# Delta rule stage: decay and beta rows by DMA, a blockwise transpose for the second inverse, one product for keys with keys and queries

## The reference

```python
cum = jnp.cumsum(g, axis=-1)
decay = jnp.exp(jnp.where(causal, cum[..., :, None] - cum[..., None, :], -jnp.inf))
k_beta = k * beta[..., None]
a = jnp.where(strict, jnp.einsum('bhnid,bhnjd->bhnij', k_beta, k) * decay, 0.0)
rhs = jnp.concatenate([v * beta[..., None], k_beta * jnp.exp(cum)[..., None]], axis=-1)
sol = lax.linalg.triangular_solve(a + eye, rhs, left_side=True, lower=True, unit_diagonal=True)
u, w = sol[..., :dv], sol[..., dv:]
attn = jnp.einsum('bhnid,bhnjd->bhnij', q, k) * decay
q_dec = q * jnp.exp(cum)[..., None]
k_dec = k * jnp.exp(cum[..., -1:] - cum)[..., None]
def step(state, xs):
    v_new = u_c - jnp.einsum('bhck,bhkv->bhcv', w_c, state)
    o = jnp.einsum('bhck,bhkv->bhcv', q_c, state) + jnp.einsum('bhij,bhjv->bhiv', attn_c, v_new)
    state = state * last_c[..., None, None] + jnp.einsum('bhck,bhcv->bhkv', k_c, v_new)
    return state, o
```

## Time and profile before

| | us |
|---|---|
| median of 3 runs | 4228.07 (4224.93 to 4230.5) |
| the profiled execution | 4243.35 |
| its span, first to last instruction | 4241.6 |
| delta rule rounds 0 to 8 in it | 2069 to 3003 |
| a full round (start of one `keys_twice` copy on POOL to the next) | 118.5 to 123.2 |

### The profile page before, as it was taken

How to read it: one execution, slowest core, us unless ns; L and a number is a source line. 1 busy time by engine, 2 the same in 40 slices (tenths; PEclk the granted TensorE clock), 3 DMA queues, 4 the chain that set the end, 5 groups by cost and what they waited for, 6 DMA issues and landing times.

```text
span 4241.6 us, 62565 instructions
## 1 busy us (share of the span) xinstructions
PE 3905.2 (92%) x25559; PEld 3618.2 (85%) x25559; DVE 2563.3 (60%) x5015; ACT 1553.4 (37%) x2769; POOL 754.8 (18%) x613
## 2 busy tenths in 40 slices
PE   7999989889979999998899999999889999978999
PEld 5667869889979999988798888889789998978999
DVE  4654337889958999998455555555453423555342
ACT  4554223335533333333433333332242424444231
POOL 0000005556722333331211101111000001110000
PEclk9999999999989999999789999999899999998999
DMA  3112224448869999996001111110022221112221
GB/s 110 60 60 70 90 75 131 135 147 283 277 213 326 336 333 332 327 330 219 25 26 31 36 39 33 36 36 31 31 81 85 95 70 46 60 45 71 93 90 66
DMA packets 203069, 528.19 MB, mean 125 GB/s; under 512 B 17032, under 2 KB 91272, under 8 KB 202784
## 3 DMA queue, kind: packets, MB, share of 16 engines
q1 hardware_dynamic: 99792, 341.22, 24.1%
q0 software_dynamic: 37440, 136.33, 9.1%
q10 hardware_dynamic: 65552, 46.64, 3.5%
HBM read 477.99 MB, written 46.14 MB: 124 GB/s over the span
## 4 chain that ended last, share of the span: by engine, by line
PE 64%; DVE 24%; ACT 6%; issue 3%; DMA 1%; POOL 0%; DVEq 0%; ACTq 0%; POOLq 0%; SPq 0%
PE bank L94 63%; DVE wl L121 5%; DVE acc L131 3%; DVE H L121 2%; DVE row L163 2%; ACT wh L115 2%; DVE yc L131 1%; DVE eq L121 1%; PE bank L97 1%; DVE aal L121 1%; DVE fs L121 1%; DMA raw<-in_v 1%; DVE sq L131 1%; ACT Xh L115 1%; DVE Xl L121 1%
## 5 line engine op out<-in xcount | busy, mean ns | idle before, releaser
L94 PE MATMUL bank<-Xh,wh 128*128 128x272 f32 (+3 forms) x3680 | 1242.1, 338 | 63.1 <-ACT ft L115 27.0
L94 PE MATMUL bank<-Xl,wh 128*128 128x272 f32 (+3 forms) x3680 | 1174.0, 319 | 0.0
L94 PE MATMUL bank<-Xh,wl 128*128 128x272 f32 (+3 forms) x3680 | 1172.4, 319 | 0.0
L121 DVE TENSOR_TENSOR wl<-raw,wh 128x1024 fp32r<-128x1024 f32 (+1 forms) x536 | 574.4, 1090 | 463.9 <-ACT wh L115 462.8
L115 ACT ACTIVATE wh<-raw 128x1024 fp32r<-128x1024 f32 (+1 forms) x632 | 589.1, 953 | 700.1 <-PE bank L94 659.6
L94 PEld LDWEIGHTS bank<-Xh,wh 128*128 128x128 f32 x3680 | 720.1, 196 | 133.2 <-issue 63.9
L94 PEld LDWEIGHTS bank<-Xh,wl 128*128 128x128 f32 x3680 | 718.4, 195 | 21.0
L94 PEld LDWEIGHTS bank<-Xl,wh 128*128 128x128 f32 x3680 | 721.0, 196 | 17.0 <-issue 0.3
L121 DVE TENSOR_TENSOR H<-H,bank 128x384 f32<-128x384 f32 (+3 forms) x522 | 252.4, 493 | 339.0 <-PE bank L94 335.4
L94 PE MATMUL bank<-aah,wh 128*128 128x384 f32 x1024 | 356.1, 348 | 43.5 <-DVE wl L121 23.5
L121 POOL TENSOR_TENSOR wl<-raw,wh 128x1024 fp32r<-128x1024 f32 x96 | 274.3, 2859 | 518.5 <-ACT wh L115 518.4
(11 more groups left out here) (309 smaller groups left out, 6404.8 us busy)
## 6 DMA issues: line engine op xcount, KB each, us to landing
raw<-in_u SPq DMA_DIRECT2D x128, 512.0 KB, 4.1
raw<-in_v SPq DMA_DIRECT2D x128, 512.0 KB, 5.8
raw<-in_up SPq DMA_DIRECT2D x64, 512.0 KB, 3.6
raw<-in_down SPq DMA_DIRECT2D x64, 512.0 KB, 3.5
scratch<-gb ACTq DMA_DIRECT2D x12, 2048.0 KB, 13.8
gj<-scratch SPq DMA_DIRECT2D x32, 768.0 KB, 7.3
raw<-in_w_gdn SPq DMA_DIRECT2D x48, 512.0 KB, 3.5
raw<-in_w_att SPq DMA_DIRECT2D x36, 512.0 KB, 3.5
```

Source lines behind the costliest of these rows:

```text
L94: return Issued(self, self.q and self.q.matmul(out, l, r, start=start, stop=stop), 1)
L121: return Issued(self, self.q and self.q.tensor_tensor(out, a, b, op), 1)
```

## The change

It makes three edits in the levels, and an order that goes with them.

1. Rows by DMA. After the gates, ACT writes the rows of cumulated gates, of their exponentials and of the betas to a scratch tensor in HBM (`rows_out`). SP reads them back, spread over 128 partitions: `rows_in(p, g)` straight into DD and QE, `beta_in(p, g)` into one of the two `sq` buffers that the norms use elsewhere. PE's `decay` and the beta part of `pair_kk` are gone, ACT's exponential into TA and POOL's mask step too; DVE subtracts the column and adds the mask with one instruction a chunk (nine of 128x128 in place of three of 128x384), POOL multiplies the queries into QE in place.
2. One product. Keys and queries lie interleaved in one tile QK, and one matmul a chunk with the weights KD2 gives both, 128 columns.
3. The second inverse by transposes. "pd", its subtraction, and `level0` on PE and ACT are gone. After each update of TB, DVE transposes it in blocks of 32x32 into TA (`squares`, STREAM_TRANSPOSE, 128x384), five times a group. Blocks of up to 32 are all that levels 1 to 5 read.

The levels have 37 units of weight in `merge` in place of 45. Cut to its core:

```diff
+    def squares(self, out, in_):
+        return Issued(self, self.q and self.q.transpose(out, in_), 1)
...
-        QS = Ring([alloc("q", 9, 64) for _ in range(2)])
-        KS = Ring([alloc("k", 9, 64) for _ in range(3)])
+        QK = alloc("qk", 5, 9, 64)
+        QS = Ring([QK[:, i, :, :] for i in (1, 3)])
+        KS = Ring([QK[:, i, :, :] for i in (0, 2, 4)])
...
+            for p in range(2):
+                for g in range(3):
+                    rows_in(p, g)
+            beta_in(0)
+            beta_in(1)
...
         def levels_gdn(p):
-            DD.take(p), TB.take(p), KE.take(p), QE.take(p)
+            TB.take(p), KE.take(p)
             do("keys_twice", p)
             for g in range(3):
-                PA.take(("dec", p, g))
                 do("decay", p, g)
-                PA.give(("dec", p, g), ("dd", p, g, 0))
+            yield 1
+            for g in range(3):
+                for n in ("kk", "vt"):
+                    PA.take((n, p, g))
+                do("pair", p, g)
+                PA.give(("kk", p, g), ("attn", p, g))
+                PA.give(("vt", p, g), ("bv", p, g))
+                SQ.give(("beta", p, g), ("bb", p, g, 1))
+                beta_in(3 * p + g + 2)
                 yield 1
...
+                if c % 3 == 2 and p < 6:
+                    rows_in(p + 2, c // 3)
...
-                streams.append((levels_gdn(t - 1), 45))
+                streams.append((levels_gdn(t - 1), 37))
...
+            def pair(p, g):
                 ps = PS[clear(pe, PA, ("kk", p, g))]
                 pe.wait_ge("kd", p)
-                k = KS.at[p]
+                pe.wait_ge("qk", p, 0, 1)
+                first, second = sorted((2 * KS.slot[p], 2 * QS.slot[p] + 1))
                 for n in range(3):
-                    i = pe.mm(ps[:, n * 64:n * 64 + 64], KD2[:, 3 * g + n, :], k[:, 3 * g + n, :])
+                    i = pe.mm(ps[:, n * 128:(n + 1) * 128].rearrange("p (e i) -> p e i", e=2),
+                              KD2[:, 3 * g + n, :], QK[:, first:second + 1:second - first, 3 * g + n, :])
...
             def decay(p, g):
+                dd = DD.at[p]
+                dv.wait_ge("dup", 1, 1)
+                dv.wait_ge(f"rows{(3 * p + g) % 2}", p, g, 1)
+                for c in range(3 * g, 3 * g + 3):
+                    dv.stt(dd[:, c, :], dd[:, c, :], CC[:, c, p:p + 1], CS["mask"], ALU.subtract, ALU.add).then_inc(
+                        "dd", p, c)
...
+                dv.wait_ge("tmm", p, lv, g)
+                dv.tt(to, to, pt, ALU.subtract).then_inc("tb", p, lv, g)
                 if lv < 5:
-                    dv.wait_ge("dmm", p, lv, g)
-                    less("pd", "dmm", TA, 0).then_inc("ta", p, lv, g)
-                dv.wait_ge("tmm", p, lv, g)
-                less("pt", "tmm", TB.at[p], b).then_inc("tb", p, lv, g)
+                    dv.wait_ge("tb", p, lv, g)
+                    dv.squares(three(TA, g).rearrange("p c x -> p (c x)"), tb).then_inc("ta", p, lv, g)
...
+            def rows_in(p, g):
+                m = 3 * p + g
+                name = f"rows{m % 2}"
+                if p < 2:
+                    sp.wait_ge("dup", 3, 1)
+                    sp.wait_ge("nbe", 0)
+                    sp.wait_ge("rows_out", 2)
+                else:
+                    sp.wait_ge("so", p - 2, 3 * g + 2)
+                if m > 1:
+                    sp.wait_ge(name, (m - 2) // 3, (m - 2) % 3, 1)
+                for i, x in enumerate((DD.at[p], QE.at[p])):
+                    sp.dma(three(x, g), scratch3[i, 3 * g:3 * g + 3, 2 * p:2 * p + 2, :].rearrange(
+                        "c h i -> c (h i)").partition_broadcast(128)).then_inc(name, p, g, i)
```

More of the change, by code:

```diff
@@ L318, in __init__, with build @@
         self.name, self.i = name, i
-def build(nc, X, out, scratch, scratch2):
+def build(nc, X, out, scratch, scratch2, scratch3):
     ctx = ExitStack()
@@ L1178, in build, with beta_in @@
         QE, DD, TB, KE = (Ring([alloc(n, 9, 128) for _ in range(2)], given=gates_done) for n in ("qe", "dd", "tb", "ke"))
+        for pair in range(8):
+            QE.at[pair], DD.at[pair] = QE.bufs[pair % 2], DD.bufs[pair % 2]
+        def rows_in(p, g):
+            do("rows_in", p, g)
+        def beta_in(m):
+            if m < 24:
+                SQ.take(("beta", m // 3, m % 3))
+                do("beta_in", m // 3, m % 3)
         assert top[0] >= end
@@ L1311, in levels_gdn @@
         def levels_gdn(p):
[L1312 removed]
+            TB.take(p), KE.take(p)
             do("keys_twice", p)
             for g in range(3):
[L1315 removed]
                 do("decay", p, g)
[L1317 to L1333 removed]
+            yield 1
[7 more added lines that the diff above has]
+                beta_in(3 * p + g + 2)
+                yield 1
+            QS.give(p, ("kk", p, 2), ("qe", p, 2))
             for g in range(3):
@@ L2022, in pe_program @@
                 onehot=onehot, ba=ba,
-                gdn_dup=gdn_dup, decay=decay, pair_kk=pair_kk, pair_kq=pair_kq, keys_out=keys_out, level0=level0,
+                gdn_dup=gdn_dup, pair=pair, keys_out=keys_out,
                 level_x=level_x, level_t=level_t, scan_r=scan_r, scan_v=scan_v, scan_s=scan_s, ml_if=ml_if,
@@ L2807, in decay, with rows_out @@
             def decay(p, g):
[L2808 to L2820 removed]
+                ac.wait_ge("dd", p, 3 * g + 2)
+                ac.act(three(DD.at[p], g), three(DD.at[p], g), ACT.Exp).then_inc("dd_exp", p, g)
+            def rows_out():
+                ac.wait_ge("cum", 0)
+                ac.act(RR[1], CUM, ACT.Exp).then_inc("ecum", 0)
+                ac.wait_ge("ecum", 0)
+                for i, x in enumerate((CUM, RR[1], RB)):
+                    ac.dma(scratch3[i].rearrange("c h i -> h c i"), x).then_inc("rows_out", i)
             def scan_v(p, c):
@@ L3001, in decay, with pair @@
             def decay(p, g):
-                dd = DD.at[p]
-                po.wait_ge("dd", p, g, 0)
-                po.tt(three(dd, g), three(dd, g), b3(CS["mask"]), ALU.add).then_inc("ddm", p, g)
-            def pair_kq(p, g):
-                qe = clear(po, QE, p)
+                qe = QE.at[p]
                 q = QS.at[p][:, 3 * g:3 * g + 3, :].unsqueeze(2).to_broadcast([128, 3, 2, 64])
                 po.wait_ge("qk", p, 0, 1)
-                po.wait_ge("ec", p, g)
-                po.tt(four(qe, g), q, four(TA, g), ALU.mult).then_inc("qe", p, g)
-            def keys_out(p, g):
+                po.wait_ge(f"rows{(3 * p + g) % 2}", p, g, 1)
+                po.tt(four(qe, g), q, four(qe, g), ALU.mult).then_inc("qe", p, g)
+            def pair(p, g):
                 tb = clear(po, TB, p)
@@ L3185 @@
     scratch2 = nc.dram_tensor("scratch2", (4 * AHEAD, 128, NT), F32, kind="Internal").ap()
-    build(nc, X, out, scratch, scratch2)
+    scratch3 = nc.dram_tensor("scratch3", (3, 9, 16, 64), F32, kind="Internal").ap()
+    build(nc, X, out, scratch, scratch2, scratch3)
     r = run(nc, [{"in_" + n: a for n, a in arr.items()}], core_ids=[0])
```

123 lines of the change are left out of this document (42 added, 81 removed).

## The result

The changed kernel takes 4184.32 us (median of 4 runs, 4180.28 to 4191.06), the kernel before, measured beside it, 4229.28 (4224.93 to 4232.13). The ratio is 0.9896, 95% interval 0.9879 to 0.9913: 45 us less, 1.0%. The forecast was 4118, from 4064 to 4178: right in sign, and 66 us too low.

What follows compares the result with a forecast made beforehand. The prediction took TensorE (PE) to bound the levels stage; 133 us off PE, less 16 for new waits, 2 for betas and 5 for the first pair, made 110 us off: 4118 us, range 4064 to 4178.

Steps and rivals of the forecast that it cites:

- PE's work: Full levels round: removed products, row broadcasts, transposes and changes between matmul kinds take 16.7 us off PE, 133 us in eight rounds.
- The decays of pair p + 2 are fetched a round ahead: hidden at either price.: Row DMAs on SP: decay rows cost no time, whether a landing takes 3.5 or 11.6 us.
- I take 3.5: Row DMAs of 192 KB: 3.5 us a landing; group 2's betas cost 2 us in all, the first pair 5 us once.
- Rival D: Row DMAs land late, at 11.6 us, at group 2's betas and the first pair: 95 us more, 4213; chance 0.07.
- The new waits: PE waiting for DVE, mainly at a round's start: 2 us a round, bounds -1.7 and +5; 16 us in eight rounds.
- Rival C: DVE's lumps of in-order work bite: new PE waits of 8 us a round in place of 2, 4166; chance 0.16.
- The closing of the sum: Whole kernel: 133 - 16 - 2 - 5 = 110 us off the profiled 4243.35, then 15.3 us to the median: 4118.
- DVE's transpose: Blockwise transposes of 128x384, 15 a round on DVE: 0.556 us each, 8.3 us a round.
- Rival B: PE's clock rises too: half of the 77 us lost to half clock goes, no new waits, 4064; chance 0.16.
- Rival E: Slower: new 2.2 us waits drop PE's clock, 10 us each; two more a round make 160 us, 4278; chance 0.07.
- What the profile was to show: Levels rounds of 104 to 109 us, 757 matmul records, 120 STREAM_TRANSPOSE of 0.5 to 0.6 us, PE waits 5 to 9 us.
- Both signs of being wrong: Levels stage: the prediction is wrong if rounds stay over 115 us or PE's share of the stage falls under 90%.

Runs made afterwards that it cites:

- the late order: Changed kernel with the third group's decay and pair steps moved behind the second group's keys, three steps later, same work: 4128.37 us, ratio 0.9757 to the kernel before.

## Why the prediction was wrong, point by point

**PE's work: right.** 16.1 us a round measured, 16.7 summed. Of it 8.6 belong to the transposes (8.4 and entries summed). The joint product of 128 columns takes 0.67 us from its start to the next row's (2504.93 to 2505.60), as taken.

**"The decays of pair p + 2 are fetched a round ahead: hidden at either price." This is the step that failed.** The call in the diff stands behind every third chunk of the scan of pair p, and that scan ends one round before the round in which the levels of pair p + 2 start. SP's queue in the round before the one shown above:

```profile
2457.98 0.38 SPq L176 DMA_DIRECT2D dd<-scratch  x1
...
2481.77 0.38 SPq L176 DMA_DIRECT2D dd<-scratch  x1
```

With the levels' round starting at 2501.2, group 0 is fetched 43 us ahead, group 1 19 us, and group 2, at 2507.02, not at all. The scan doesn't hold it that long. PE's last row for the output product of chunk 8:

```profile
2499.96 0.56 PE L95 MATMUL bank<-qe,st 128*128 128x64 f32 x4
```

It is done at 2500.5, 6.5 us before the rows are issued. In between SP stands at two weight fetches that come first in its queue and wait for DVE's splits; they go at 2505.37 and 2506.6, and the rows right behind. I had read the distance for the pair and not for each group, and had looked at weight fetches behind rows, not at rows behind weight fetches. At the same 7.1 us (2507.02 to 2514.13) rows issued at 2500.5 would be there at 2507.6, before DVE is ready for them at 2508.1: an estimate from these rows, since no run puts them ahead of the weight fetches. With a landing of 6.7 us and a bank behind ACT's queue the late issue ends in a wait of 9 us a round. Taking away that landing alone gave 33 us, the other order 54.

**"I take 3.5" us a landing, from the weights of 512 KB.** 4.7 in the median for one tile of betas, 6.7 for a pair of decay tiles, 11.7 for the first betas. The median was not hidden where nothing stood between issue and use. The 11.6 us, taken for the worst, is the median of tiles of 768 KB in the earlier trace rows; the first betas just passed it. Rival D had this mechanism in the wrong places: at the betas of group 2 nothing shows in full rounds. At the start PE's wait of 24 us lies between the 5 us taken and D's 35.

**The new waits: 2 us a round taken, 10.6 measured** (16.4 less 5.8), beyond the upper bound of 5 as well. That bound was made of doubled present waits. The wait that came stands at the same step as that for dd, the values' transpose, but ACT's ro gives the bank back, and a second wait for ro follows; the earlier trace rows had none for ACT. Without the late landing 5.6 us a round would still be new, where 2 were taken, so this term was too small by itself. Rival C's 8 us was the nearest number. Its cause, DVE's load, was wrong: 74 us a round was forecast rightly, and 6.9 us more of it costs 2 to 3 us. What part its lump at the start of a round has in the 5.6 us stays open.

**The closing of the sum,** in the traces, from the start of the first levels' round to that of the eighth, before and after:

```profile
2086.90:2903.00 816.10, 780.41 (x5793) 726.97 (x5792) 446.30 (x922) 279.51 (x582) 109.73 (x122) 0.92 0.11 33
```

```profile
2085.50:2842.90 757.40, 636.39 (x4929) 596.02 (x4928) 486.80 (x984) 262.28 (x540) 93.11 (x100) 0.92 0.20 54
```

PE's busy time falls by 144 us, of which 7 x 16.1 = 113 are work. The other 31 I put down to half clock that no longer stretches it: the clock's mean is the same, but part of the half clock lies in the waits (0.70 in the 9 us above, 0.61 in the 24 us of the first pair). Its idle time rises from 36 to 121, by 85 us. 144 less 85 is 59, and 4 more came outside these rounds: 63. In the forecast idle time was to rise by 23 in all, the clock to give nothing. Of the 66 us between 4118 and 4184, 19 are the executions that happened to be profiled: I took off 15.3 us for before, and after lay 4 us below its own median.

**DVE's transpose: right.** 576 ns for the 556 taken. The Trainium skill, "VectorE: DVE Perf Modes", The three transpose paths, gives 311 ns for 128x128 bf16, from which three made an estimate of 0.93 us for this tile; the trace does not bear that out for the fp32 tile of 128x384. The run with the level transposes doubled had DVE's load of that estimate, 81 us a round, and lost 2 to 3 us a round by it.

**Rival B: the clock did rise, but in other kernels.** In the kernel with the transposes alone it is 0.98 to 1.00 in full rounds, though no wait went; I can't say why from these runs. In the late order it is 0.97 to 1.00. **Rival E** is not borne out: in the changed kernel two more waits of over 2.2 us a round left the mean clock at 0.92.

**What the profile was to show.** 757 records, no rows of xr,tb for pd, STREAM_TRANSPOSE of 0.5 to 0.6 us x120: held. Rounds of 104 to 109 and waits of 5 to 9 us, all for DVE: not held in the changed kernel, and nearly held, at 103.2 to 106.3 and 8.1 to 9.7 us, in the late order, though ACT is waited for there too. Both signs of being wrong came: a round of 115.5 us, and PE at 84% of the stage (636.39 of 757.4 us).

## What to carry to other kernels

When a broadcast by the matmul engine is replaced by a prefetched transfer, find the place of each issue by itself, in the queue that issues it, what the issues ahead of it there wait for, and its distance to the first reader, group by group: "a round ahead" was 43 us for the first group, 19 for the second and nothing for the third. Then follow who stands behind that reader in its engine's order, since the wait surfaces two engines away, under the name of the last one to release. And measure the parts of a change apart: here one part brought 81 us, and the others took 36 of them back, until the same transfers were put in another order.

## What the runs showed of the hardware that was not expected

**The same wait with and without a drop of the clock.** The earlier trace rows had half clock for 16.5 us behind a wait of 2.2 us for rc. The same wait, of 2.17 us at the same place, is followed by none in the changed kernel, nor in the one with the transposes alone. Windows before and behind it, of the changed kernel and then of the one with transposes alone:

```profile
2440.00:2457.80 17.80, 14.72 (x123) 13.44 (x121) 13.36 (x26) 5.58 (x11) 0.00 (x0) 1.00 0.10 30
2457.90:2474.40 16.50, 16.50 (x138) 15.50 (x139) 7.76 (x17) 4.56 (x12) 0.00 (x0) 1.00 0.28 88
```

```profile
2427.60:2445.60 18.00, 14.91 (x124) 13.63 (x123) 13.46 (x27) 5.11 (x10) 0.00 (x0) 1.00 0.10 30
2446.70:2463.20 16.50, 16.50 (x141) 15.58 (x141) 8.56 (x19) 3.79 (x10) 0.00 (x0) 1.00 0.17 61
```

PE's work ahead of it is alike in all three (14.7 to 14.9 us of about 18). In the trace of before itself the clock is at 0.50 for 17 us behind this wait in two full rounds, and for 6.7 and 6.8 us in two others (2359.5 to 2366.2 and 2724.6 to 2731.4). What makes the drop stays open; the price of a wait (rival E's 10 us for each 2.2) can't be read from one instance.

**Transposes and subtractions on DVE.** A blockwise transpose of 128x384 fp32 takes 576 ns, hardly more than a masked copy of the same tile from PSUM (552 to 556). The subtraction with a column and a mask took 446 ns in the mean for 128x128, where the row it was costed by had 349; its median is 340, and single ones took up to 1193 ns. There are nine of over 1.1 us, and each starts within 0.05 us of POOL's product qe<-qk,qe, released by the same landing; the other 63 take 0.34 us at most.

**Landing grows with what is in flight.** 192 KB spread to 128 partitions in 512-byte pieces, each time from a tile's own issue to its landing: 4.7 us in the median for the single tiles of betas, 6.7 us for the second of a pair issued together, and 11.5 us for the last of the four that open the stage (2098.71 to 2110.2).
